# A two-layer hybrid decoder step on one NeuronCore: the first feed-forward block by plain products, and one Winograd sum moved between two convolutions

## The reference, cut to what matters

```python
x = x + jnp.einsum('blm,md->bld', mix, w['w_out'][l])
h = _rmsnorm(x, w['norm_ffn_g'][l])
gu = jnp.einsum('bld,df->blf', h, w['ffn_w_up'][l])
gate, up = gu[..., :D_FF], gu[..., D_FF:]
gate, ffn_buf = _causal_dwconv(gate, st_ffn_conv[l], w['ffn_conv_w'][l], w['ffn_conv_b'][l])
x = x + jnp.einsum('blf,fd->bld', jax.nn.gelu(gate) * up, w['ffn_w_down'][l])
```

## Time and profile before

| | us |
|---|---|
| median of 3 runs | 2851.26 (2850.53 to 2852.26) |
| the profiled execution | 2852.5 |
| its span, first to last instruction | 2850.6 |
| PE busy | 2735.3 (96%) |
| DVE busy | 1978.6 (69%) |
| POOL busy | 1308.0 (46%) |
| ACT busy | 867.3 (30%) |
| mean granted TensorE clock | 0.982 |

### The profile page before, as it was taken

The page is one execution under the profiler, slowest core; times in us unless marked ns, Lnnn a source line. Parts: engine busy times, 40 slices in busy tenths (PEclk is TensorE's granted clock), DMA queues, the critical chain, the costliest instruction groups (busy, mean ns, idle before and its releaser), DMA issues.

```text
span 2850.6 us, 52195 instructions
## 1 busy us (share of the span) xinstructions
PE 2735.3 (96%) x19254; PEld 2668.2 (94%) x19254; DVE 1978.6 (69%) x2478; ACT 867.3 (30%) x1392; POOL 1308.0 (46%) x766
## 2 busy tenths in 40 slices
PE   9999999987999999999999999998979999999997
PEld 8999999886999999999999999998879999999997
DVE  7658886368677666666846597855688666666678
ACT  4333231124332223222413342211233223223323
POOL 2333333214756556666433333231147556666663
PEclk9999999998999999999999999999989999999998
DMA  4325334410111111111223344244101111111112
GB/s 159 131 69 167 122 100 166 148 42 23 46 52 52 54 49 44 44 58 46 71 82 102 115 131 142 100 156 143 32 23 54 58 45 44 44 59 44 44 54 94
DMA packets 76414, 228.67 MB, mean 80 GB/s; under 512 B 18736, under 2 KB 19888, under 8 KB 75200
## 3 DMA queue, kind: packets, MB, share of 16 engines
q1 hardware_dynamic: 71888, 211.25, 22.6%
q10 hardware_dynamic: 4368, 15.33, 1.7%
HBM read 181.10 MB, written 45.96 MB: 80 GB/s over the span
## 4 chain that ended last, share of the span: by engine, by line
PE 53%; issue 17%; DVE 14%; POOL 11%; DMA 2%; ACT 1%; DVEq 0%; POOLq 0%; SPq 0%; ACTq 0%
PE ps L889 16%; PE ps L891 15%; PE ps L890 15%; POOL sb_w_lo L785 7%; DVE sb_fpt L2458 2%; DVE sb_pt L1892 2%; DVE sb_x L1882 1%; DMA sb_w_raw<-w 1%; POOL sb_w_raw L835 1%; POOL sb_wsum L824 1%; POOL sb_w_raw L831 1%; DVE sb_ch L1960 1%; PE ps L1118 1%; POOL sb_w_raw L827 1%; PE ps L1024 1%
## 5 line engine op out<-in xcount | busy, mean ns | idle before, releaser
L785 POOL TENSOR_TENSOR sb_w_lo<-sb_w_raw,sb_w_hi 128x512 fp32r<-128x512 f32 (+1 forms) x352 | 650.0, 1849 | 470.8 <-ACT sb_w_hi L1680 463.2
L889 PE MATMUL ps<-sb_p_hi,sb_w_hi 128*128 128x258 f32 (+1 forms) x2560 | 736.7, 288 | 47.9 <-POOL sb_w_lo L785 35.1
L891 PE MATMUL ps<-sb_p_hi,sb_w_lo 128*128 128x258 f32 (+1 forms) x2560 | 731.1, 286 | 0.0
L890 PE MATMUL ps<-sb_p_lo,sb_w_hi 128*128 128x258 f32 (+1 forms) x2560 | 730.1, 285 | 0.0
L782 POOL TENSOR_TENSOR sb_w_hi<-sb_w_raw,sb_ones 128x1024 fp32r<-128x1024 f32 (+1 forms) x92 | 181.8, 1976 | 918.1 <-PEq L886 821.0
L889 PE MATMUL ps<-sb_h_hi,sb_w_hi 128*128 128x344 f32 x1632 | 534.6, 328 | 10.5 <-DVE sb_x L1882 6.2
L889 PEld LDWEIGHTS ps<-sb_p_hi,sb_w_hi 128*128 128x128 f32 x2560 | 488.4, 191 | 55.0 <-issue 47.2
L890 PE MATMUL ps<-sb_h_lo,sb_w_hi 128*128 128x344 f32 x1632 | 523.1, 321 | 0.0
L891 PE MATMUL ps<-sb_h_hi,sb_w_lo 128*128 128x344 f32 x1632 | 521.7, 320 | 0.0
L889 PE MATMUL ps<-sb_y_hi,sb_w_hi 128*128 128x344 f32 x1440 | 478.6, 332 | 22.5 <-DVE sb_x L1882 14.3
L890 PEld LDWEIGHTS ps<-sb_p_lo,sb_w_hi 128*128 128x128 f32 x2560 | 489.7, 191 | 0.0
(11 more groups left out here) (310 smaller groups left out, 3741.3 us busy)
## 6 DMA issues: line engine op xcount, KB each, us to landing
sb_w_raw<-w SPq DMA_DIRECT2D x178, 512.0 KB, 3.6
proj<-sb_ev SPq DMA_DIRECT2D x64, 516.0 KB, 3.0
sb_rawx<-w SPq DMA_DIRECT2D x44, 512.0 KB, 3.5
sb_pt<-proj SPq DMA_DIRECT2D x28, 516.0 KB, 4.9
sb_raw<-proj SPq DMA_DIRECT2D x16, 516.0 KB, 4.6
sb_raw<-proj ACTq DMA_DIRECT2D x16, 516.0 KB, 4.2
sb_ch<-cumT SPq DMA_DIRECT2D x32, 256.0 KB, 4.1
sb_raw<-ssd_state SPq DMA_DIRECT2D x4, 1024.0 KB, 6.3
```

The lines of the kernel that those rows point to most:

```text
L785: return nc.gpsimd.tensor_tensor(o, a, h.bitcast(F32), ALU.subtract)
L889: mm(o, wh, ah, start=first, stop=False)
L890: mm(o, wh, al, start=False, stop=False)
L891: return mm(o, wl, ah, start=False, stop=last)
```

## The change

Block 0 no longer uses the seven-product scheme. Its four tiles are computed by `plain_tile`, 8 k-steps x 3 column groups x 3 matmuls of 344 columns each, from row panels of gain times x. The panel order in memory changes so that a row's two halves lie in neighbouring panels: rows 0 to 3 in the places of I1 and I4, rows 4 to 7 in those of I2 and I3. So I1, I2 and I3 are there with the rows, and I4 can be written only when the plain products have read rows 0 to 3. DVE now makes, while the mixer's last pieces come, only the sums of squares and the row remainders; ACT makes squares and rounded rows. The difference panels I5, I6, I7 are made later, by `panels(kk)` for kk 0 to 3, and I4 by `fourth(kk)`, in between the work on block 0. The temporary pieces lie in the two halves of tab. POOL's three square sums and its eight weight sums of block 0 go away; block 0 has 8 weight entries, not 14. PE makes the token sums behind plain tile 0 and spreads rstd inside plain tile 1. In the looped and the last block c11 of the second pair is put between the two convolutions, the scaling by rstd of the first gelu tile behind c12, and that of the second behind down piece 0 (in the last block behind times_gelu(0)). The last y goes into I7 in place of I3.

```diff
-I1, I2, I6, I5, I7, I4, I3 = range(7)
-PER_BLOCK, LAST_ENTRIES = 18, 22
+I1, I4, I6, I5, I2, I3, I7 = range(7)
+FIRST_ENTRIES, PER_BLOCK, LAST_ENTRIES = 8, 18, 22
...
+    def plain_bank(n):
+        return ps[:, 4:7, :] if n % 2 == 0 else ps[:, 0:3, :]
...
+    def h_cols(t, k, g):
+
+        at = (I1 if k < 4 else I2) * 4 * H + (k % 4) * H
+        if g == 0:
+            return flat(t)[:, at:at + TG]
+        if g == 2:
+            return flat(t)[:, at + 4 * H + 2 * TG - H:at + 5 * H]
+        step = 4 * H - TG
+        return flat(t)[:, at + TG:at + TG + 2 * step].rearrange("p (a n) -> p a n", a=2)[:, :, 0:TG // 2]
+
+    def h_row(t, k):
+        i = I1 if k < 4 else I2
+        return t[:, i:i + 2, k % 4, :]
...
-                taken(b, -2)
+                taken(b, -3)
...
-            for m, a in ((1, raw[:, 0, 2:T + 2]), (2, tab[:]), (3, raw[:, 0, 2:T + 2])):
-                pool.wait_ge(*sg.after("sqf_tile", m))
-                if m > 1:
-                    pool.wait_ge(*sg.after("sqf_pool", m - 1))
-                nc.gpsimd.tensor_tensor(rstd[:], rstd[:], a, ALU.add).then_inc(*sg.on("sqf_pool", m))
...
-            up_pair(None, 0)
-            up_pair(None, 1)
+            for e in range(FIRST_ENTRIES):
+                lo(None, e, f_place(e // 2)[:, 512 * (e % 2):512 * (e % 2) + 512])
...
+            def plain_tile(j):
+                o = plain_bank(j)
+                if j >= 2:
+                    pe.wait_ge(*seen("f_ev", layer, None, j - 1))
+                for k in range(KD):
+                    e = 2 * j + k // 4
+                    if k % 4 == 0:
+                        entry_ready(None, e)
+                    if j == 0:
+                        pe.wait_ge(*sg.after("pn_lo", ("h", k)))
+                    w = slice(k % 4 * P, k % 4 * P + P)
+                    for g in range(NG):
+                        og = o[:, g, 0:TG].rearrange("p (a n) -> p a n", a=2) if g == 1 else o[:, g, 0:TG]
+                        ins = three(og, w_place(w_hi, e)[:, w], w_place(w_lo, e)[:, w], h_cols(p_hi, k, g),
+                                    h_cols(p_lo, k, g), k == 0, k == KD - 1)
                         weights_done()
-                ins.then_inc(sg.sem("f_done"), 1)
-
-            def mixer_left(bank0):
-                for b_ in range(bank0, bank0 + 2):
-                    last = max(r for r in RING.values() if r % NB == b_)
-                    pe.wait_ge(*sg.after(f"p_free{b_}", last))
-
-            def ffn_sums():
-                pe.wait_ge(*sg.after("sqf_dve", KD - 1))
-                pe.wait_ge(*seen("f_ev", layer, None, 1))
-                for c in range(NCH + 1):
-                    s = slice(c * CHUNK, min((c + 1) * CHUNK, T))
-                    ins = mm(ps[0:s.stop - s.start, 2, c:c + 1], rstd[:, s], ones[:, 0:1], start=True, stop=True)
-                ins.then_inc(*sg.on("tok_sum", "ffn"))
-
-            def ffn_spread():
-                pe.wait_ge(*sg.after("tok_rstd", "ffn"))
-                pe.wait_ge(*seen("f_ev", layer, None, 5))
-                for c in range(NCH + 1):
-                    n = min(CHUNK, T - c * CHUNK)
-                    o = ps[:, 6, 0:8] if c == NCH else ps[:, 4 + c // 4, (c % 4) * CHUNK:(c % 4) * CHUNK + n]
-                    ins = mm(o, rt[0:n, c:c + 1].to_broadcast([n, P]), ident[0:n, 0:n], start=True, stop=True)
-                ins.then_inc(*sg.on("tok_spread", "ffn"))
+                    if k % 4 == 3:
+                        ins.then_inc(sg.sem("f_done"), 1)
+                    if j == 1 and k == 3:
+                        spread_rstd("ffn")
...
+            plain_tile(0)
+            for b_ in range(NB):
+                last = max(r for r in RING.values() if r % NB == b_)
+                pe.wait_ge(*sg.after(f"p_free{b_}", last))
+            token_sums("ffn")
+            for j in range(1, 4):
+                plain_tile(j)
...
+            def hi_row(m):
+                af(h_row(p_hi, m), x[:, m, :].rearrange("p (a n) -> p a n", a=2), ACT.Identity,
+                   scale=gf[:, m:m + 1]).then_inc(*sg.on("pn_hi", ("h", m)))
...
+            for m in range(KD):
+                x_done(m)
+                square_f(m)
+                hi_row(m)
+                if m == 5:
+                    hi(None, 0)
+                    hi(None, 1)
...
+            def scale_t1(kk):
+                act.wait_ge(*sg.after("pn_t", (I5, kk)))
+                af(ta, ta, ACT.Identity, scale=gf[:, kk:kk + 1]).then_inc(*sg.on("pn_s", kk))
+                act.wait_ge(*sg.after("pn_s", kk))
+                hi_t(I5, kk, ta)
+
+            def panels(kk):
+                scale_t1(kk)
+                hi_t(I6, kk, tb)
+                hi_t(I7, kk, ta)
...
+                if pair == 0:
+                    act.wait_ge(*sg.after("pn_lo", (I4, 3)))
...
+            panels(0)
+            hi(None, 3)
+            panels(1)
+            root("ffn")
+            hi(None, 4)
+            tap(None, 0, "first", 0)
+            hi(None, 5)
+            panels(2)
+            hi(None, 6)
+            gelu("first", 0)
+            tap(None, 0, "first", 1)
+            panels(3)
+            hi(None, 7)
+            gelu("first", 1)
+            hi(0, 0)
+            hi(0, 1)
+            hi_t(I4, 0, ta)
+            hi_t(I4, 1, tb)
+            hi(0, 2)
+            hi_t(I4, 2, ta)
+            hi_t(I4, 3, tb)
...
+            def square_add(m):
+                dve.wait_ge(*sg.after("sqf_tile", m))
+                if m == 0:
+                    v.tensor_copy(rstd[:], raw[:, 0, 2:T + 2]).then_inc(*sg.on("sqf_used", 0))
+                else:
+                    dve.wait_ge(*sg.after("sqf_used", m - 1))
+                    v.tensor_tensor(rstd[:], rstd[:], raw[:, 0, 2:T + 2] if m % 2 == 0 else tab[:],
+                                    ALU.add).then_inc(*sg.on("sqf_used", m))
+
+            def lo_row(m):
+                dve.wait_ge(*sg.after("pn_hi", ("h", m)))
+                stt(h_row(p_lo, m), x[:, m, :].rearrange("p (a n) -> p a n", a=2), gp(m), h_row(p_hi, m).bitcast(F32),
+                    ALU.mult, ALU.subtract).then_inc(*sg.on("pn_lo", ("h", m)))
...
+            def panels(kk):
+                dve.wait_ge(*(sg.after("pn_lo", (I7, kk - 1)) if kk else sg.after("sqf_used", KD - 1)))
+                v.tensor_tensor(ta, x[:, kk, n1], x[:, kk, n0], ALU.subtract).then_inc(*sg.on("pn_t", (I5, kk)))
                 dve.wait_ge(*sg.after("pn_s", kk))
+                stt(tb, x[:, 4 + kk, n1], gp(4 + kk), ta, ALU.mult, ALU.subtract).then_inc(*sg.on("pn_t", (I6, kk)))
+                lo_t(I5, kk, ta)
+                dve.wait_ge(*sg.after("pn_lo", (I5, kk)))
+                stt(ta, x[:, kk, n0], gp(kk), tb, ALU.mult, ALU.subtract).then_inc(*sg.on("pn_t", (I7, kk)))
+                lo_t(I6, kk, tb)
+                lo_t(I7, kk, ta)
+
+            def fourth(kk):
+                t = (ta, tb)[kk % 2]
+                dve.wait_ge(*(sg.after("pn_lo", (I4, kk - 2)) if kk > 1 else sg.after("pn_lo", (I7, 3))))
+                stt(t, x[:, 4 + kk, n0], gp(4 + kk), p_hi[:, I6, kk, :].bitcast(F32), ALU.mult,
+                    ALU.subtract).then_inc(*line.step())
+                dve.wait_ge(*line.last())
+                v.tensor_tensor(t, t, p_lo[:, I6, kk, :].bitcast(F32), ALU.subtract).then_inc(*sg.on("pn_t", (I4, kk)))
...
+            for mo in range(4, KD):
+                for g in range(NG):
+                    evict(("fin", mo, g))
+                square_add(mo - 1)
+                lo_row(mo - 1)
+            square_add(KD - 1)
+            lo_row(KD - 1)
             dve.wait_ge(*sg.after("small_stored", (5, 1)))
             for j in range(2):
                 v.memset(raw[:, j, 0:2], 0.0).then_inc(*line.step())
                 dve.wait_ge(*line.last())
+            panels(0)
+            panels(1)
+            token_norm("ffn", ps[:, 7, 0:NCH + 1])
...
+            def plain_gate(j):
+                plain_done(j)
+                v.tensor_tensor(g3(raw[:, j, 2:T + 2]), plain_bank(j)[:, :, 0:TG], g3(rstd[:]),
+                                ALU.mult).then_inc(sg.sem("f_ev"), 1)
+                evicted(None, j + 1)
+                v.nop().then_inc(sg.sem("f_gate"), 1)
+
+            def plain_up(j):
+                plain_done(2 + j)
+                dve.wait_ge(*stored_to(j, layer, None))
+                v.tensor_tensor(g3(raw[:, j, 2:T + 2]), plain_bank(2 + j)[:, :, 0:TG], g3(fpt[:, j, :]),
+                                ALU.mult).then_inc(sg.sem("f_ev"), 1)
+                evicted(None, j + 3)
+                v.nop().then_inc(sg.sem("f_y"), 1)
...
                 conv_gate(blk, tag, 0)
+                c11(b, 1)
                 conv_gate(blk, tag, 1)
-                c11(b, 1)
-                scale_gelu(tag, 0)
                 add_p6(b, 1)
                 c22(b, 1)
                 c12(b, 1)
-                scale_gelu(tag, 1)
+                scale_gelu(tag, 0)
                 c21(b, 1)
...
```

(36 more changed lines are left out.)

225 lines of the change are left out of this document (47 added, 178 removed).

## The result

The changed kernel takes 2827.8 us (median of 4 runs, 2826.2 to 2830.4) against 2851.6 for the kernel before (4 runs); the ratio is 0.9918, 95% interval 0.9905 to 0.9930. Predicted were 2832 and a range of 2811 to 2847. A second set of 5 runs of the changed kernel gave 2827.5 and 0.9918 again. All later ratios are to runs of the kernel before on the same chip at the same time, so 0.001 is 2.85 us. The interval of each ratio reaches about 4 us to either side, so the times alone don't show a difference of less than some 5 us between two variants; there I go by marks in the traces, which are one profile of each variant.

What follows compares the result with a forecast made beforehand. PE, busy 2735 of 2850.6 us, would be held by DVE at block 0's third product; 18.6 us gained at the entry plus 0.8 from c11's move make 19.4, giving 2833.1, median 2832, range 2811 to 2847.

Steps and rivals of the forecast that it cites:

- F: End of the last residual matmul in layer 0, forecast near 682.3 us, with small residual waits gone but for some 0.3.
- DVE bounds block 0: From F to the end of plain_up(1), DVE needs 42.8 us work, 7.4 hand-overs, 13.0 port waits, ending at F + 63.3.
- Port waits: DVE operations with two SBUF inputs meeting POOL in block 0: ten lengthened by 1.25 us, one by 0.5, 13.0 in all.
- The prediction's cross-check: Entry-stretch means exceed uncrowded durations by 0.60 and 0.23 us; some 45 operations at 0.3 give the same 13.5 us.
- The waits in block 0: First looped block: PE's product 0 late by 1.0 us, product 1 by 0.4, the third product by 7.1, product 3 by 3.8.
- The clock: The 7.1 us wait in block 0 brings half-rate clock back: 1.2 us taken, bounds 0 and 5.4.
- c11 between the convolutions: Looped blocks: product 12 on time, wait moves to product 13, 0.18 us per block left, 3.2 us in 18 blocks.
- Rival C: Looped blocks: the wait for c11 really goes, entry 13 being no later; 11.7 us more, 2820 us; chance 0.12.
- the second part: Moves of c11 and the scalings: 3.2 us gained in looped blocks, 2.4 lost in the last blocks, net 0.8 us gained.
- B: Block 0: DVE at plain_up(1) by F + 56, POOL's operations falling into hand-over waits; 12.1 us more per layer, 2808; chance 0.13.
- D: Little gain left: half-rate clock at its upper bound (4.2 more per layer), block 0's waits 3 us longer; 2846; chance 0.13.
- E: DVE's port waits double to 26 us in the first block; 6.6 us slower than before, 2858; chance 0.07.

Runs made afterwards that it cites:

- second profile: Changed kernel run again unaltered, for another profile and more runs; a second set of 5 runs gave 2827.5 us, 0.9918 of the kernel before.
- e3: Against the changed kernel: POOL's splits of the plain block's weight entries 2 to 7 made on 64 of 512 columns; 2822.6 us, 0.9905 of before.
- e5: Against the changed kernel: ACT rounds weight entry 13 ahead of the second gelu, in looped and last blocks; 2816.8 us, 0.9879 of before.
- e1: Against the changed kernel: c11 of the second pair behind both convolutions again and both gelu scalings put back, in all blocks; 2826.6 us, 0.9921 of before.
- e4: Against the changed kernel: DVE makes the second plain up product straight behind the first, ahead of panel I4's four pieces; 2826.6 us, 0.9919 of before.
- e6: Against the changed kernel: third group of difference panels made before DVE's wait for spread rstd, rounded ahead of ACT's first tap; 2822.3 us, 0.9903 of before.
- e12: Against the changed kernel: e5 and e1 together, so entry 13 early but c11 and both scalings at their old places; 2841.1 us, 0.9966 of before.
- e2: Against the changed kernel: in the last block alone, the scaling of the second gelu tile stands before c21 again; 2823.8 us, 0.9906 of before.

## Why the prediction was right, point by point

**The residual phase and F: right.** The last residual matmul ends 37.0 us behind the first (680.2 - 643.16), in the second profile 35.8 and 36.9; predicted 682.3 - 645.0 = 37.3. The small waits are gone altogether.

**PE to the first Winograd product: right.** 50.3 us from F to product 0, predicted 49.1 + 1.0. The 5.2 us of additional arithmetic were paid and no plain tile waited.

**DVE bounds block 0: right in kind, its terms partly off.** plain_up(1) (740.58 below) ends at 741.8, F + 61.6; predicted F + 63.3. The other two rows are POOL's split beside the first up product:

```profile
740.58 1.22 DVE L2456 TENSOR_TENSOR sb_raw<-ps,sb_fpt 128x1032 f32<-128x1032 f32 x1
...
728.15 1.83 POOL L800 TENSOR_TENSOR sb_w_lo<-sb_w_raw,sb_w_hi 128x512 fp32r<-128x512 f32 x1 [3.31 <-ACT sb_w_hi L1682]
729.03 1.23 DVE L2456 TENSOR_TENSOR sb_raw<-ps,sb_fpt 128x1032 f32<-128x1032 f32 x1 [0.22 <-DVE sb_fpt L2437]
```

The terms:
- Work 43.1 us against 42.8 predicted.
- Hand-overs 8.6 against 7.4: the spread took 3.0 instead of 2.2, the waits for ACT's scaling 4.4 together (4.8 predicted), the rest are small waits of DVE for itself that I hadn't counted.
- **Port waits 9.9 us against 13.0: this is the term that was mis-sized.** Eleven operations are longer than their free duration, by 0.44 to 1.06 us each, and not by 1.25: POOL's operation has always begun a little earlier. POOL pays as well: its split at 728.15 and the sum at 722.69 last 1.83 and 2.15 us instead of 1.27. The Trainium skill, "SBUF — State Buffer", section "Who interferes with whom", states that a DVE instruction with at most one SBUF input, outside the 2-port perf modes, does not contend with GpSimd, and that one with two does, against a GpSimd instruction that reads SBUF. The trace agrees: all eleven have two, and the product out of PSUM at 729.03 lasts 1.23 us beside POOL's split of 728.15.
- The prediction's cross-check did not bear out its 13.0 us. Its two groups exceed the uncrowded durations by 0.60 us (12 operations) and 0.23 us (8), which is 0.45 on average and 20 us for 45 operations, not 13.5. The measured 9.9 us are 0.22 for each of 45.

e3 shows a second fault of that step, which the sum hides: I added all port waits into one chain to plain_up(1). Those ahead of the spread (1.9 us) cost nothing, because DVE would have waited there instead.

**The waits in block 0: the two long ones in the right places, all forecast 0.4 to 1.6 us too long.** Printed are 0.5, 0, 5.5 and 2.2 us against 1.0, 0.4, 7.1 and 3.8. The 0.5 us of product 0 are ended by DVE's first up product (L2456), not by the weight entry behind the second gelu that I had named. Product 3 comes 12.3 us earlier (105.5 us behind the first residual matmul, before 762.83 - 644.99 = 117.8), predicted 10.5. Of the difference of 1.8, 1.7 is DVE's earlier end.

**The clock: it falls as forecast, its price is not shown apart.** Behind the 5.5 us wait the granted clock is 0.66, 0.84 and 0.82 on three windows of 5 us in the changed kernel:

```profile
740.00:745.00 5.00, 2.98 (x14) 2.99 (x15) 4.55 (x6) 1.53 (x3) 0.10 (x1) 0.66 0.01 2
...
750.00:755.00 5.00, 5.00 (x37) 5.00 (x37) 1.39 (x2) 0.63 (x1) 2.13 (x2) 0.82 0.32 108
```

Product 4 starts 4.37 us behind product 3 instead of 2.88, 1.5 us where I had taken 1.2. In the second profile it is 3.0, but there product 10 waits 0.5 us for POOL, which it doesn't in the first. From product 3 to product 12 the two layers take 27.5 and 27.4 us in the first profile, 27.3 and 27.1 in the second, 26.2 before: 0.9 to 1.3 us more, near the 1.2 forecast, once with a half-rate stretch behind product 3 and once with hardly any there.

**c11 between the convolutions: the mechanism was right, two prices off.** Product 12 is on time, product 13 waits 0.2 to 0.6 us for POOL, because of ACT's order, and 0.2 to 0.25 us per block are left; predicted 0.18. Rival C (the wait truly goes, 11.7 us more) was false as it stood, and e5 gives it: once entry 13 is ahead of the gelu, 11 us. In the last block the wait for the first down piece rises from 1.10 to 2.29, by the 1.2 predicted. Not foreseen: up to 1.7 us of half-rate clock behind it, and 1.6 us in the final norm. So I had the second part at +0.8 us; by the marks it is 4.3 - 3.9 - 1.6 = -1.2, and e1 measures none.

**The rivals.** B (the cover holds) fell: DVE was at plain_up(1) at F + 60.4, not F + 56, and e4 shows that even then I4 and ACT's row behind it hold the fourth product. D fell since the clock cost at most 1.5 and not 5.4 us; E, since 9.9 us of port waits are not 26. The forecast was 4 us too high. By the marks of the first profile the entry gave 22.2 us for 18.6 and the looped blocks 1.1 more than forecast; the last blocks and the final norm took back 1.5 and 1.6 more, and 1.7 came from the mixers, which the change doesn't touch. That these last four nearly cancel is luck. Most of the rest is the median, 2.6 us under the profiled execution where I had taken 1.2.

## What to carry to other kernels

When one engine's list sets the time, mark in it each wait for an engine that keeps its own time, here the spread: only what stands behind the last such wait shortens the end (e3), and work moved into the wait costs nothing there, though it may uncover another wait at its old place (1.4 of 3.8 us in e6). A move that takes away one wait shows its worth only with the next one: c11's place alone gave nothing net, entry 13's place without it cost 13 us (e12 against e1), the two together gained 12 (e5 against e1). Before work is moved on a shared engine, look in every period of the loop at what will run beside it, not only in the stretch that is to be mended.

## What the hardware showed that was not expected

- **A short wait costs more than it prints.** In the changed kernel product 13 starts 3.50 us behind product 12, not 2.88: 0.62 us for a printed wait of 0.47. The block is 0.73 us longer than in e5, which has none. Over 18 blocks the printed waits are 3.7 + 3.8 us; taking them away gave 11.
- **Half-rate clock of some 1.5 us comes and goes in unchanged code.** The stretch of 550 to 560 us is short of full clock (0.66 or 0.83) in twelve of the fourteen profiles and at full clock in two, the first of the changed kernel and e5. Product 0 stands 85.8 to 87.3 us behind the first residual matmul in the fourteen layers of seven profiles (changed kernel twice, e1, e2, e4, e5, e12) whose code is the same up to there and whose waits are too. The difference lies in the residual phase, 35.5 to 35.8 or 36.9 to 37.0 us long; from its end to product 0 all fourteen take 50.3. A single profile can't settle 2 us.
- **DVE and POOL lengthen each other**, in either order of start: 2.34 for 1.27 us on DVE when POOL's split starts 0.03 us earlier, and 1.83 to 2.15 for 1.27 on POOL when DVE holds the port. A 0.23 us operation on 8 columns takes 1.0 us in such a place.
